# A hybrid decoder trunk on one core: the first mixer's triangular inverses with both token halves in turns over four quadrants of TensorE, their masks on GpSimd

## The chip, the core and the metric

One Trainium2 chip, one of its cores. The time is the device time of one launch in microseconds. The kernel before has a median of 1386.16 us over three runs (1382.22 to 1388.61).

## What is computed

The reference is a two-layer decoder trunk on 256 tokens of width 1024, all in float32. Layer 0 has a hybrid mixer: an RWKV-7 head group (8 heads of 64) and a sparse-attention head group (8 query heads, compressed, selected and sliding-window branches), whose outputs are joined and projected. Layer 1 has a Mamba-2 mixer. After each mixer comes a mixture of experts (32 experts of width 512, each token goes to two), and after all a final norm. The change touches the RWKV group only:

```python
def step(state, inp):                       # per token, per head
    r_t, w_t, k_t, v_t, a_t, b_t = inp
    sa = jnp.einsum('bhij,bhj->bhi', state, a_t)
    state = state * w_t[:, :, None, :] + sa[..., None] * b_t[:, :, None, :] + v_t[..., None] * k_t[:, :, None, :]
    return state, jnp.einsum('bhij,bhj->bhi', state, r_t)
...
y = y * gn_w + gn_b
bonus = jnp.sum(r_h * k_h * r_k, -1, keepdims=True) * v_h
y = y.astype(cols.dtype) + bonus.reshape(b_, s_, RWKV_WIDTH)
return y * g
```

## The kernel before

The kernel has one block per stage: `hyb` (the first mixer), experts of layer 0, `ssm` (the Mamba-2 mixer), experts of layer 1, the final norm. In a block each engine has its own stream of instructions, written out by hand; `at(...)` turns the name of a mark into a semaphore and a count, and an engine waits for it. There is no planner: the order of the calls is the order on the engine.

**The recurrence in chunks.** RWKV's recurrence is done in four chunks of 64 tokens (two per half of 128 tokens, `t`, and in it `q` = 0 or 1). For each chunk and head a strictly lower triangular 64x64 matrix N comes from a and b, and (1 - N) is inverted. There are 2 halves x 8 heads = 16 slots (`slot(t, e, c)`, head 2c + e), and in each slot chunk q lies in partitions 64q to 64q + 63 (`at64(q)`). `tri` (in `amt`) is the inverse as grown so far, `triT` (in `kk`) its transpose, both 128 x 16 x 64. Level 0 comes from the masks `lev0` and `levT`; each of the five levels l = 1 to 5 then doubles the blocks: `products(l)` (PE) multiplies `lv` (the level's masked part of N, `masked`, L799) with `tri` into `prod`; ACT copies `prod` out of PSUM (`products_read`, L1057); `grown(l)` on PE multiplies `triT` with `prod` (dT) and `prod` with `triT` (dTT, both in `squares`, L1360), and `grown(l)` on DVE adds them to `tri` and `triT` (L810). The last level has no dT.

**On PE** a matmul of 64 x 64 uses one quadrant of the array: its rows go by the partitions of the inputs, its columns by those of the output. In `squares` both are `at64(q)`, so a run of them uses two quadrants, on the diagonal. `against` (L1322, for `bar` and `kar`) and the `nn` matmuls (L1334) read at `at64(e)` and write at `at64(q)`. The profile has two records for each float32 matmul and one for a transpose.

**In turns with attention.** The attention group's selected and window branches are eight units i = 0 to 7 (`UNITS`; 128 keys wide for i = 0 to 3, 256 for i = 4 to 7). Unit i goes: `scores(i)` on PE (L1242), `scores(i)` on DVE (scale and mask L626, maximum L631), `exps(i)` on ACT (L938, four heads), `weighted(i)` on DVE (reciprocal L640, L641, product L644), `weights_turned(i)` on PE (transposes, L1155), `weights_read(i)` on ACT (L948), and for each pair of units `attended` on PE (L1265). Level l and unit l share a stretch, in this order on each engine (levels 3 to 5 alike but for akv, the turned compressed weights and attended):

```python
# PE, level 4                          # DVE                        # ACT
weights_turned(4)                      scores(5)                    attention_read(0)
scores(5)                              masked(4)                    weights_read(4)
products(4)                            pre = pre * gate             products_read(4)
grown(4)                               weighted(5)                  exps(5)
                                       grown(4)
```

PSUM has eight banks: attention takes its jobs from banks 0 to 2 in turn (`inner`), the inverse from banks 4 to 7 (`right`); `take` (L189) hands out the next bank of the pool and waits until its last job has been read. DVE also builds `pre` (bonus times v, plus `gn_b`, times the gate; L826, L834, L842) and scales `gate` by `gn_w` (L847).

After level 5 come `wu` (L1443; the inverse times its right sides, copied by ACT for e = 0 and by DVE for e = 1), `gains` (L1454, L1456) and `queries` (L1465), the step from chunk to chunk (`step`, `carried`), the group norm on DVE, and the join: on PE the output projection in 64 matmuls of 512 columns (L1535 for the attention half, L1544 for the RWKV half after `turnr`).

**DMA.** SP loads the experts' weights of layer 0 ahead into a ring of 24 slots of 1 MB, as the mixer's buffers come free: it waits for `gup`, `attended(3)`, `qs(1, 1)` and `turnr(1)` in turn (L565 to L576), and in the experts' block for the router. GpSimd has no work in this block; in `ssm` it has 14 instructions (L2302, L2310, L2312).

## Time and profile before

| | us |
|---|---|
| median of three runs | 1386.16 |
| the profiled execution | 1384.46 |
| its span (first to last instruction) | 1382.7 |
| PE busy | 1252.7 (91%) |
| DVE busy | 408.8 (30%) |
| ACT busy | 269.8 (20%) |
| GpSimd (POOL) busy | 15.2 (1%) |
| DMA, bytes moved | 464 MB, mean 336 GB/s |

The page also cuts the span into 40 slices of 34.6 us. The first mixer takes slices 1 to 7; DMA is busy in nine tenths of the time or more in slices 8 to 20 and 29 to 40, the two expert stages, and in few tenths in most of slices 2 to 6. PE is the modelled busy time of matmuls, PEld that of weight loads, PEclk the TensorE clock that was granted (1.00 is 2.4 GHz, 0.50 is 1.2 GHz). An "idle before" with an arrow names what ended an engine's wait.

### The profile page before, as it was taken

The numbers are of one execution on the slowest core, as the hardware profiler recorded it, in microseconds if no ns is written. First come the engines' busy times: TensorE is split into PE (matmuls) and PEld (weight loads), VectorE is DVE, ScalarE is ACT, GpSimd is POOL, SyncE is SP. The second block draws the span as 40 slices with busy tenths as digits, with TensorE's granted clock in tenths as the row PEclk, the third lists the DMA queues.
The fourth block names the chain that finished last, engine by engine and source line by source line (L and its number), as shares of the span: only waits on it lengthen the run. The fifth ranks groups of instructions, "written<-read, shape, count | busy, mean of one in ns | idle before, by whom it ended". The sixth has DMA issues, their size and how long they took to land. (4 is left out here: it accounts for less than half of the span.)

```text
span 1382.7 us, 20783 instructions
## 1 busy us (share of the span) xinstructions
PE 1252.7 (91%) x8752; PEld 701.5 (51%) x8752; DVE 408.8 (30%) x1019; ACT 269.8 (20%) x537; POOL 15.2 (1%) x18
## 2 busy tenths in 40 slices
PE   7999999899999888598899999998999998877986
PEld 4678874444444433243378888544444453333432
DVE  1158764511112111112135756224211211110211
ACT  2241440311110100010132566112111010000101
POOL 0000000000000000000000111000000000000000
PEclk9999999999999999889999999999999999997999
DMA  9620128999999999999964455958999999999996
GB/s 305 189 95 28 64 82 354 404 428 428 428 425 429 427 427 427 426 426 428 369 219 169 152 212 199 366 230 327 427 428 427 428 427 428 427 426 426 427 428 264
DMA packets 63482, 464.08 MB, mean 336 GB/s; under 512 B 8272, under 2 KB 13680, under 8 KB 34960
## 3 DMA queue, kind: packets, MB, share of 16 engines
q1 hardware_dynamic: 63376, 462.61, 81.8%
q8 instruction: 73, 1.20, 0.4%
q14 instruction: 33, 0.27, 0.1%
HBM read 461.51 MB, written 1.08 MB: 335 GB/s over the span
## 5 line engine op out<-in xcount | busy, mean ns | idle before, releaser
L1982 PE MATMUL bank<-raw,xg 128*32 128x512 f32 x1664 | 233.6, 654 | 46.9 <-DMA raw<-in_moe_w_up 41.1
L1892 DVE TENSOR_TENSOR aT<-bank,sg 128x128 f32<-128x128 f32 (+1 forms) x64 | 20.2, 316 | 553.9 <-ACT sg L1803 553.9
L1982 PEld LDWEIGHTS bank<-raw,xg 128*32 128x32 f32 x1664 | 57.9, 119 | 196.6 <-issue 122.0
L1919 PE MATMUL bank<-sel,ux 128*128 128x64 f32 (+1 forms) x896 | 117.7, 287 | 17.0 <-DVE sel L1825 16.1
L1919 PEld LDWEIGHTS bank<-sel,ux 128*128 128x128 f32 x896 | 110.9, 202 | 40.7 <-issue 21.6
L2029 PE MATMUL sums<-ys,selT 64*128 64x512 f32 x512 | 127.2, 615 | 3.3 <-DVE ys L1905 3.3
L1800 ACT COPY gus<-bank 128x512 f32<-128x512 f32 x64 | 37.5, 586 | 439.5 <-PE bank L1982 332.1
L2020 PE MATMUL bank<-raw,aT 128*32 128x512 f32 x832 | 100.0, 598 | 10.8 <-DVE aT L1892 10.8
L2029 PEld LDWEIGHTS sums<-ys,selT 64*128 64x128 f32 x512 | 44.1, 186 | 87.8 <-issue 80.9
L1963 PE MATMUL bank<-raw,xg 128*64 128x512 f32 x384 | 87.0, 594 | 0.0
L2623 PE MATMUL sums<-uT,wr 128*128 128x256 f32 x352 | 78.1, 380 | 0.0
L1905 DVE COPY ys<-bank 128x512 f32<-128x512 f32 x64 | 44.0, 688 | 111.6 <-PE bank L2020 79.8
L1993 PEld LDWEIGHTS bank<-cst,gus 128*128 128x128 f32 x416 | 50.3, 191 | 44.5 <-issue 34.9
L2623 PEld LDWEIGHTS sums<-uT,wr 128*128 128x128 f32 x352 | 66.3, 190 | 9.4 <-issue 0.7
L1993 PE MATMUL bank<-cst,gus 128*128 128x64 f32 x416 | 57.5, 281 | 4.2 <-ACT gus L1800 4.2
L1774 ACT COPY xg<-bank 128x256 f32<-128x256 f32 (+1 forms) x56 | 23.4, 418 | 177.9 <-PE bank L1919 177.9
L1963 PEld LDWEIGHTS bank<-raw,xg 128*64 128x64 f32 x384 | 32.2, 137 | 49.2 <-issue 44.9
L2623 PE MATMUL bank<-uT,wr 128*128 128x256 f32 x256 | 57.1, 381 | 0.0
L2623 PEld LDWEIGHTS bank<-uT,wr 128*128 128x128 f32 x256 | 48.0, 190 | 6.9 <-issue 0.7
L2020 PEld LDWEIGHTS bank<-raw,aT 128*32 128x32 f32 x832 | 21.7, 109 | 50.6 <-issue 30.4
L2007 PE MATMUL bank<-raw,aT 128*64 128x512 f32 x192 | 43.8, 598 | 3.0 <-DVE aT L1892 3.0
L1803 ACT ACTIVATE sg<-bank 128x128 f32<-128x128 f32 (+1 forms) x64 | 19.1, 298 | 137.7 <-PE bank L1993 114.8
(414 smaller groups left out, 1282.4 us busy)
## 6 DMA issues: line engine op xcount, KB each, us to landing
raw<-in_moe_w_gate SPq DMA_DIRECT2D x54, 2048.0 KB, 41.7
raw<-in_moe_w_up SPq DMA_DIRECT2D x54, 2048.0 KB, 46.1
raw<-in_moe_w_down SPq DMA_DIRECT2D x54, 2048.0 KB, 45.0
raw<-in_moe_w_gate SPq DMA_DIRECT2D x20, 1024.0 KB, 11.2
raw<-in_moe_w_up SPq DMA_DIRECT2D x20, 1024.0 KB, 12.7
raw<-in_moe_w_down SPq DMA_DIRECT2D x20, 1024.0 KB, 12.4
wr<-in_ssm_w_in SPq DMA_DIRECT2D x10, 2048.0 KB, 8.1
wr<-in_hyb_w_in SPq DMA_DIRECT2D x5, 2048.0 KB, 7.9
```

Source lines behind the costliest of these rows:

```text
L1774: nc.scalar.copy(dst[:, :, 4 * half:4 * half + 4, :].rearrange("p x k s -> p k x s"), bank[SIDE_BANK][:, 0:8 * n].rearrange("p (k x s) -> ...
L1800: nc.scalar.copy(gus[:, :, :], bank[GU_BANK][:, :].rearrange("p (q j) -> p j q", j=4)).then_inc(S["gus"], 1)
L1892: V.tensor_tensor(out, bank[TURN_BANK][:, 0:8 * n].rearrange("p (j x) -> p j x", j=4)[:, :, n:2 * n], gated, ALU.mult).then_inc(S["act"], 1)
L1905: V.tensor_copy(ys[:, :], bank[Y_BANK][:, :]).then_inc(S["y"], 1)
L1919: i = T.matmul(bank[SIDE_BANK][:, k * n:(k + 1) * n].rearrange("p (x s) -> p x s", x=2), ux[:, t, 4 * half + k, :], src[:, t, :, :], start ...
L1963: i = T.matmul(bank[GU_BANK][CAP * m:CAP * m + CAP, :], xg[:, odd, k, :], raw[:, slot, (k % 4) * FH:(k % 4 + 1) * FH], start=(k == 0), sto ...
L1982: i = T.matmul(bank[GU_BANK][CAP_S * c:CAP_S * c + CAP_S, :], xg_f[:, x, 4 * half + k, :], raw[:, slot, k * FH:(k + 1) * FH], start=(half ...
L1993: i = T.matmul(bank[TURN_BANK][:, j * CAP:(j + 1) * CAP], gus[:, j, :], C("ident64"), start=True, stop=True)
L2007: i = T.matmul(bank[Y_BANK][CAP * n:CAP * n + CAP, :], aT[:, j, :], raw[:, slot, jj * D + n * BANK:jj * D + (n + 1) * BANK], start=(j == 0 ...
L2020: i = T.matmul(bank[Y_BANK][CAP_S * c:CAP_S * c + CAP_S, :], aT_s[:, 2 * half + jj, :], raw[:, slot, jj * D + n * BANK:jj * D + (n + 1) * ...
L2029: i = T.matmul(bank[ACC[2 * t + n]][:, :], selT[CAP * n:CAP * n + CAP, x, t * P:(t + 1) * P], ys[CAP * n:CAP * n + CAP, :], start=False, s ...
L2623: i = T.matmul(b[:, c * SEQ:(c + 1) * SEQ], wr2[:, n % 3, k, (2 * j + c) * P:(2 * j + c + 1) * P], uT2[:, k, :], start=(k == 0), stop=(k = ...
```

## The change

Both halves' matmuls now alternate. `tri` stays where it is for both halves; for the second half `triT`, `prod`, the a side and akv lie in the other 64 partitions (chunk q in `at64(1 - q)`). Then `products` and dT use two quadrants for the first half and the other two for the second; dTT keeps to the diagonal for both. The second half of `triT` starts from new matmuls (`crossed`), and at(1) is formed by matmuls with the identity. `products(l)` now stands first in its stretch on PE and `products_read(l)` ahead of `weights_read(l)` on ACT. akv, wu, gains and queries alternate likewise. DVE adds both dT ahead of both dTT. The masks and the steps of `pre` and `gate` go to GpSimd; SP and DVE wait for its last (`gain`). The diff, cut to its core:

```diff
             sp.wait_ge(*at("attended", 3))
+            sp.wait_ge(*at("gain"))
             load_ahead(sp, 0, hyb_fed, hyb_attended)
...
             go(V.tensor_tensor(lv[:, 1], nrb[:, :, 0, :], rep(levT[:, 1], SL), ALU.mult), "lvl", 1)
-            did(V.tensor_tensor(triT, nrb[:, :, 0, :], rep(levT[:, 0], SL), ALU.mult))
+            go(V.tensor_tensor(triT[:, 0:HEADS, :], nrb[:, 0:HEADS, 0, :], rep(levT[:, 0], HEADS), ALU.mult))
+            dve.wait_ge(*at("crossed"))
+            for e in range(2):
+                go(V.tensor_tensor(triT[:, slot(1, e, 0):slot(1, e, 4), :],
+                                   bank_of("crossed", e)[:, 0:4 * CHK].rearrange("p (c s) -> p c s", s=CHK),
+                                   rep(levT[:, 0], 4), ALU.mult), "read", "crossed", e)
+            dve.wait_ge(dve_done, DV.n)
...
             def grown(l):

-                for g in range(2):
-                    for name, dst in (("dT", tri), ("dTT", triT)):
-                        if name == "dT" and l == LAST:
-                            continue
+                for name, dst in (("dT", tri), ("dTT", triT)):
+                    if name == "dT" and l == LAST:
+                        continue
+                    for g in range(2):
                         dve.wait_ge(*at(name, l, g))
                         sl = dst[:, HEADS * g:HEADS * g + HEADS, :]
                         go(V.tensor_tensor(sl, bank_of(name, l, g)[:, :].rearrange("p (c s) -> p c s", s=CHK), sl,
...
             weighted(1)

             scores(2)
-            masked(1)
             compressed_turned(0)
             weighted(2)
             grown(1)

             scores(3)
...
-            masked(2)
-            dve.wait_ge(*at("read", "bon"))
...
             weighted(3)
...
             scores(4)
-            masked(3)
-            dve.wait_ge(*got("par"))
...
             compressed_turned(1)
             weighted(4)
...
             scores(6)
-            go(V.tensor_tensor(gate[:, :, :], gate[:, :, :], rep(gn_w, HALVES), ALU.mult))
             weighted(6)
             grown(5)
...
+            dve.wait_ge(*at("gain"))
...
+        @block.gpsimd
...
+            def masked(l):
+
+                pool.wait_ge(*(at("prod", l - 1, 1) if l > 1 else at("lvl", 1)))
+                go(G.tensor_tensor(lv[:, (l + 1) % 2], nrb[:, :, 0, :], rep(levT[:, l + 1], SL), ALU.mult), "lvl", l + 1)
+
+            masked(1)
+            pool.wait_ge(*at("read", "bon"))
+            pool.wait_ge(*at("read", "vt", 1))
+            heads_ = lambda ap: ap.rearrange("p t (n i) -> p (t n) i", i=HD)
+            go(G.tensor_tensor(heads_(pre), heads_(vt), rep(bon[:, :, :].rearrange("p t n -> p (t n)"), HD, 2), ALU.mult))
+            masked(2)
+            pool.wait_ge(*got("par"))
+            pool.wait_ge(pool_done, PO.n)
+            go(G.tensor_tensor(pre, pre, rep(gn_b, HALVES), ALU.add))
+            masked(3)
+            pool.wait_ge(*at("read", "gup", 1))
+            pool.wait_ge(pool_done, PO.n)
+            go(G.tensor_tensor(pre, pre, gate[:, :, :], ALU.mult))
+            masked(4)
+            pool.wait_ge(pool_done, PO.n)
+            go(G.tensor_tensor(gate[:, :, :], gate[:, :, :], rep(gn_w, HALVES), ALU.mult), "gain")
...
             def products_read(l):

                 for g in range(2):
-                    act.wait_ge(*at("prod", l, g))
+                    act.wait_ge(*at("prod", l, 1))
                     if l > 1:
-                        act.wait_ge(*at("dTT", l - 1, g))
+                        act.wait_ge(*at("dTT", l - 1, 1))
                     A.copy(prod[:, HEADS * g:HEADS * g + HEADS, :],
                            bank_of("prod", l, g)[:, :].rearrange("p (c s) -> p c s", s=CHK)).then_inc(
...
             by_slot("at", xr_[:, :, 0, :], 1)
+            products_read(1)
             weights_read(1)
-            products_read(1)
...
             pe.wait_ge(*at("rt"))
             against("bar", bh)
+            bs = [take(pe, "crossed", e, pool=right) for e in range(2)]
+            for c in range(4):
+                for e in range(2):
+                    for q in range(2):
+                        i = T.matmul(bs[e][at64(1 - q), c * CHK:(c + 1) * CHK],
+                                     bh[at64(e), c, chunk(1, q)], ar[at64(e), c, 0, chunk(1, q)], start=True, stop=True)
+            i.then_inc(pe_done, PE.one(("crossed",)))
             pe.wait_ge(*at("rk"))
             b = take(pe, "bon", pool=right)
...
-            for t in range(HALVES):
-                turned(("at", t), [ar[:, c, 0, tok(t)] for c in range(4)], right)
-
...
+            turned(("at", 0), [ar[:, c, 0, tok(0)] for c in range(4)], right)
+            b = take(pe, "at", 1, pool=right)
+            for c in range(4):
+                for q in range(2):
+                    i = T.matmul(b[at64(1 - q), c * P:(c + 1) * P], ar[:, c, 0, chunk(1, q)], ident, start=True,
+                                 stop=True)
+            i.then_inc(pe_done, PE.one(("at", 1)))
...
+            def squares(bs, left_, right_, source, to):
+
+                for n in range(HEADS):
                     for q in range(2):
-                        i = T.matmul(b[at64(q), s * CHK:(s + 1) * CHK], left_[at64(q), HEADS * g + s, :],
-                                     right_[at64(q), HEADS * g + s, :], start=True, stop=True)
+                        for g in bs:
+                            i = T.matmul(bs[g][at64(to(g, q)), n * CHK:(n + 1) * CHK],
+                                         left_[at64(source(g, q)), HEADS * g + n, :],
+                                         right_[at64(source(g, q)), HEADS * g + n, :], start=True, stop=True)
                 return i
+
+            straight = lambda g, q: q
+            crossed = lambda g, q: q if g == 0 else 1 - q

             def products(l):

                 pe.wait_ge(*at("lvl", l))
                 if l == 1:
                     pe.wait_ge(*at("triT0"))
+                else:
+                    pe.wait_ge(*at("read", "dT", l - 1, 1))
+                bs = {g: take(pe, "prod", l, g, pool=right) for g in range(2)}
+                squares(bs, lv[:, l % 2], tri, straight, crossed).then_inc(pe_done, PE.one(("prod", l, 1)))
+                new[("prod", l, 0)] = new[("prod", l, 1)]
+
+            def grown(l):
+
+                pe.wait_ge(*at("read", "prod", l, 1))
+                if l > 1:
+                    pe.wait_ge(*at("read", "dTT", l - 1, 1))
+                if l < LAST:
+                    bs = {g: take(pe, "dT", l, g, pool=right) for g in range(2)}
+                    squares(bs, triT, prod, crossed, straight).then_inc(pe_done, PE.one(("dT", l, 1)))
+                    new[("dT", l, 0)] = new[("dT", l, 1)]
                 for g in range(2):
-                    if l > 1:
-                        pe.wait_ge(*at("read", "dTT", l - 1, g))
-                    squares(take(pe, "prod", l, g, pool=right), g, lv[:, l % 2], tri).then_inc(
-                        pe_done, PE.one(("prod", l, g)))
-
-            def grown(l):
-
-                for g in range(2):
-                    pe.wait_ge(*at("read", "prod", l, g))
-                    for name, left_, right_ in (("dT", triT, prod), ("dTT", prod, triT)):
...
-                        squares(take(pe, name, l, g, pool=right), g, left_, right_).then_inc(
-                            pe_done, PE.one((name, l, g)))
-
+                    squares({g: take(pe, "dTT", l, g, pool=right)}, prod, triT, crossed, crossed).then_inc(
+                        pe_done, PE.one(("dTT", l, g)))
+
+            products(1)
             weights_turned(1)
             scores(2)
-            products(1)
             pe.wait_ge(*at("zz", 11))
             for t in range(HALVES):
                 turned(("vt", t), [v4[:, c, tok(t)] for c in range(4)], right)
             compressed_turned(0)
             grown(1)
...
+
+            products(2)
             attended(0)
-
             weights_turned(2)
             scores(3)
-            products(2)
             compressed_out(0)
...

+            products(3)
             weights_turned(3)
             scores(4)
-            products(3)
             pe.wait_ge(*at("read", "vt", 1))
             pe.wait_ge(*at("read", "kar", 1, 1))
-            for t in range(HALVES):
-                b = take(pe, "akv", t, pool=right)
...
+            bs = [take(pe, "akv", t, pool=right) for t in range(HALVES)]
+            for e in range(2):
+                for c in range(4):
+                    for q in range(2):
+                        for t in range(HALVES):
+                            i = T.matmul(bs[t][at64(crossed(t, q)), (4 * e + c) * HD:(4 * e + c + 1) * HD],
                                          akr[at64(q), slot(t, e, c), 0, :], vt[at64(q), t, head(e, c)],
                                          start=True, stop=True)
-                i.then_inc(pe_done, PE.one(("akv", t)))
+            i.then_inc(pe_done, PE.one(("akv", 1)))
+            new[("akv", 0)] = new[("akv", 1)]
...
             grown(3)
+
+            products(4)
             attended(1)
-
             weights_turned(4)
             scores(5)
-            products(4)
             grown(4)
...
             compressed_out(1)
             pe.wait_ge(*at("read", "akv", 1))
             pe.wait_ge(*at("read", "at", 1))
...
+            pe.wait_ge(*at("read", "dTT", LAST, 1))
+            for e in range(2):
+                bs = [take(pe, "wu", t, e, pool=right) for t in range(HALVES)]
+                for c in range(4):
+                    for q in range(2):
+                        for t in range(HALVES):
+                            half = at64(crossed(t, q))
+                            i = T.matmul(bs[t][at64(q), 2 * c * CHK:2 * (c + 1) * CHK], triT[half, slot(t, e, c), :],
+                                         flat(xr_[half, slot(t, e, c), :, :], "x", "s"), start=True, stop=True)
+                i.then_inc(pe_done, PE.one(("wu", 1, e)))
+                new[("wu", 0, e)] = new[("wu", 1, e)]
+
+            def gains_queries(j):

                 t, q = j // 2, j % 2
-                b = take(pe, "g", j, pool=right)
+                t2, q2 = (j + 1) // 2, (j + 1) % 2
+                b, b2 = take(pe, "g", j, pool=right), take(pe, "qm", j + 1, pool=right)
                 for c in range(4):
                     for e in range(2):
...
                         o = b[at64(e), c * HD:(c + 1) * HD]
                         T.matmul(o, nrb[at64(q), slot(t, e, c), 2, :], wu[at64(q), slot(t, e, c), 1, :], start=True,
                                  stop=False)
+                        T.matmul(b2[at64(e), 2 * c * CHK:2 * (c + 1) * CHK], wu[at64(q2), slot(t2, e, c), 0, :],
+                                 flat(nrb[at64(q2), slot(t2, e, c), 1:3, :], "x", "s"), start=True, stop=True)
                         i = T.matmul(o, kt[at64(q), t, head(e, c)], vt[at64(q), t, head(e, c)], start=False, stop=True)
                 i.then_inc(pe_done, PE.one(("g", j)))
...
+                new[("qm", j + 1)] = new[("g", j)]
...
-            gains(1)
+            gains_queries(0)
             pe.wait_ge(*at("read", "wu", 1, 0))
             pe.wait_ge(*at("read", "wu", 1, 1))
-            gains(2)
-            queries(2)
-            queries(3)
+            gains_queries(1)
+            gains_queries(2)
             weights_turned(7)
```

## Rows read from the trace of the kernel before

**Rows 1.** stretches: us, busy us (records) per engine, PEclk, DMA share, GB/s
```profile
206.00:210.00 4.00, 2.04 (x68) 1.93 (x67) 2.24 (x5) 1.87 (x2) 0.00 (x0) 0.97 0.97 393
210.00:214.00 4.00, 4.00 (x29) 2.25 (x25) 3.76 (x9) 0.30 (x1) 0.00 (x0) 0.60 1.01 428
...
230.00:234.00 4.00, 4.00 (x10) 1.66 (x9) 0.69 (x1) 0.00 (x0) 0.00 (x0) 1.00 0.18 76
...
340.00:380.00 40.00, 39.75 (x268) 18.91 (x266) 5.63 (x15) 4.62 (x10) 0.00 (x0) 1.00 1.00 426
```

**Rows 2.** PE in order of time: start us, us, instruction, records, idle before
```profile
138.97 2.08 PE L1360 MATMUL sums<-amt,wr 64*64 64x64 f32 x64
...
158.56 2.08 PE L1360 MATMUL sums<-amt,wr 64*64 64x64 f32 x64
...
168.30 1.09 PE L1155 MATMUL bank<-cst,pr 128*128 128x128 f32 x8
169.73 1.13 PE L1242 MATMUL bank<-kT,qT 64*128 64x256 f32 x8 [0.33 <-ACT pT L948]
170.79 2.08 PE L1360 MATMUL sums<-amt,wr 64*64 64x64 f32 x64
...
177.37 1.09 PE L1155 MATMUL bank<-cst,pr 128*128 128x128 f32 x8 [0.77 <-DVE pr L644]
...
186.41 1.09 PE L1155 MATMUL bank<-cst,pr 128*128 128x128 f32 x8 [0.73 <-DVE pr L644]
...
189.90 3.71 PE L1443 MATMUL sums<-wr,kk 64*64 64x128 f32 x64
...
199.09 1.09 PE L1155 MATMUL bank<-cst,pr 128*128 128x128 f32 x8
...
210.89 11.67 PE L1535 MATMUL bank<-zz,qk 128*128 128x512 f32 x24
```

**Rows 3.** DVE in order of time, units 3 and 5 and the adds
```profile
149.19 0.75 DVE L626 SCALAR_TENSOR_TENSOR pr<-bank,cst_hyb 128x256 f32<-128x256 f32 x2 [1.39 <-PE bank L1242]
...
153.69 0.69 DVE L644 TENSOR_TENSOR pr<-pr,den 128x512 f32<-128x512 f32 x1
...
170.96 1.29 DVE L626 SCALAR_TENSOR_TENSOR pr<-bank,cst_hyb 128x512 f32<-128x512 f32 x2 [2.27 <-PE bank L1242]
172.28 1.22 DVE L631 TENSOR_REDUCE nmx<-pr 128x4 f32<-128x1024 f32 x1
...
176.09 1.23 DVE L644 TENSOR_TENSOR pr<-pr,den 128x1024 f32<-128x1024 f32 x1
177.23 0.68 DVE L810 TENSOR_TENSOR amt<-sums,amt 128x512 f32<-128x512 f32 x1
```

**Rows 4.** ACT in order of time: the first exponential of units 3 and 5 (one of four each)
```profile
151.60 0.40 ACT L938 ACTIVATE pr<-pr,nmx 128x128 f32<-128x128 f32 x1
...
173.54 0.51 ACT L938 ACTIVATE pr<-pr,nmx 128x256 f32<-128x256 f32 x1
```

**Rows 5.** PE in order of time: `nn` and `bar`, 32 matmuls each
```profile
116.46 1.16 PE L1334 MATMUL sums<-qk,front 64*64 64x64 f32 x64
...
125.09 1.98 PE L1322 MATMUL sums<-front,qk 64*64 64x128 f32 x64
```

**Rows 6.** groups by line, 130 to 260 us: records, busy us, mean ns, idle before
```profile
L1155 PE MATMUL bank<-cst,pr 128*128 128x128 f32 x44 | 6.6, 289 | 1.5 <-DVE pr L644 1.5
...
L1265 PE MATMUL bank<-pT,nsav 128*64 128x512 f32 x24 | 6.0, 609 | 0.0
...
L1242 PE MATMUL bank<-kT,qT 64*128 64x128 f32 x16 | 1.4, 297 | 0.0
```

**Rows 7.** GpSimd's lines in `ssm`: count, shortest/median/longest ns, first and last start
```profile
L2310 POOL TENSOR_TENSOR sq<-sq x3: 1264/1267/1671, 825.1 to 862.8; 128x512 f32<-128x512 f32 x3
...
L2302 POOL TENSOR_TENSOR front<-front,dtv x8: 1043/1090/1221, 759.8 to 835.8; 128x512 f32<-128x512 f32 x8
```

**Rows 8.** one of DVE's lines in `ssm`, alike; and it in time beside GpSimd's 759.85 to 762.13
```profile
L2348 DVE SCALAR_TENSOR_TENSOR xs__2453<-xr,feat,xs__2453 x48: 475/483/1261, 741.8 to 802.4; 128x256 f32<-128x256 f32 x48
...
761.15 1.26 DVE L2348 SCALAR_TENSOR_TENSOR xs__2453<-xr,feat,xs__2453 128x256 f32<-128x256 f32 x1
```

56 lines of the change are left out of this document (10 added, 46 removed).

## The prediction

> **What bounds the kernel now.** I read the page first. Its slices show DMA at nine tenths nearly everywhere but in the first mixer; the stretches of four and forty microseconds [rows 1] then say what a shift of the mixer is worth. At 230 to 234 us the DMA share is only 0.18: the ring's next loads wait for the transposes late in the mixer (`turnr`). Later, at 340 to 380 us, DMA stands at 1.00 and PE at 39.75 of 40. So the expert stage begins when the mixer ends and cannot make time up: I count a shift of the mixer's last join one to one in the kernel's end. In the join itself PE streams 512-wide matmuls without a gap from 210.89 us [rows 2]; everything before it counts by how it moves that start.
>
> Second, PE in order of time through the five levels [rows 2]. Levels 1 to 3 are PE's: products to products takes (158.56 - 138.97) / 2 = 9.8 us in levels 1 and 2 and 12.2 us in level 3, with no idle noted in front. Levels 4 and 5 are not: PE waits 0.77 us for DVE's `pr` before `weights_turned(5)` and 0.73 before `weights_turned(6)`. There the attention units set the period, 177.37 - 168.30 = 9.07 and 186.41 - 177.37 = 9.04 us: transposes 1.09, 0.33 for ACT to free a bank, scores 1.13, DVE scores and maximum 2.5, four exponentials 2.1, DVE weights 1.6 [rows 2, 3, 4], 8.8, and the hand-overs are the rest. The inverse's matmuls fit inside that chain. This is what I rest the forecast on.
>
> **The change, part by part.**
>
> *Four quadrants.* A level's products (64 records, 2.08 us [rows 2]) now alternate over both halves. The nearest row is `nn`, also 64 records of 64x64 whose rows go by e and columns by q: 1.16 us [rows 5]. The bounds are 1.16 (it behaves as `nn`) and 2.08 (nothing overlaps); I take 1.1, since operands and shape are `nn`'s. dT gets the same; dTT of each half stays in two quadrants. So PE sheds about 0.95 + 0.95 a level, 0.95 in level 5, 0.95 in akv, 1.7 in wu (3.71 us [rows 2] against 2.0 as `bar` with its 128 columns [rows 5]) and some 1.8 where gains and queries interleave: about 13 us in all. Added are `crossed` (32 records, 0.5 us) and, for at(1), eight matmuls of 128 columns in place of four transposes, 0.35 us. The Trainium skill, TensorE: Matmul & The Clock Gate, Part 1, says that matmuls never start closer than about 25 ns; by that floor 64 records would take 1.6 us, and each level would keep 1 us more of PE. `nn` disagrees: 1160 / 64 = 18 ns [rows 5].
>
> *The order on PE.* `products(l)` moves ahead of `weights_turned(l)`, and it waits for the two dT adds of the level before. DVE does those adds after `weighted(l)`. Queued behind products on PE are attended, weights_turned and scores; DVE, then ACT, then DVE again wait for those. The chain of a level is now a ring with everything in it: products 1.1, weights_turned, scores, DVE scores, exponentials, weights, two adds 1.2 [rows 3], products. For levels 1 and 2, 128 wide: 1.1 + 0.6 + 0.7 + 1.4 + 1.5 + 1.0 + 1.2 = 7.5 [rows 3, 4, 6], with hand-overs, v's copies in front of the exponentials in the first and attended(0) 1.0 [rows 6] in the second, 8.2 and 9.0. Level 3: 1.1 + 0.6 + 1.13 + 2.5 + 2.1 + 1.6 + 1.2 = 10.3. Level 4: attended(1) is behind products too, 1.1 + 1.0 + 1.09 + 0.33 + 1.13 + 2.5 + 2.1 + 1.6 + 1.2 = 12.1 with hand-overs, against 9.07. From products(5) to weights_turned(6) there are no adds, 10.1. Products(1) would start near 138.2 (before, weights_turned(1) stood there; crossed, at(1) and the later reads of kar put back 0.7). Sum: 138.2 + 8.2 + 9.0 + 10.3 + 12.1 + 10.1 = 187.9 for weights_turned(6), against 186.41: +1.5. The first three levels gain what PE sheds, the last two give it back.
>
> *Tail.* From weights_turned(6), PE reaches wu after 189.90 - 186.41 = 3.5 us, then needs 2.0 for it. ACT's wu copies end at about 5.8, exponentials (7) at 7.9, weights (7) at 9.6. Then gains_queries(2) needs banks that DVE reads only after weighted(7) (S and mt of 1): +1.0, and +1.05 for itself; weights_turned(7) starts 11.7 after weights_turned(6), against 12.68 [rows 2]: -1.0. So the earlier PE work is hidden by the exponentials again. Order alone: +0.5 us; the hand-overs leave it open by 1.5 either way.
>
> *Masks and gains on GpSimd.* DVE loses four masks and four more 1024-wide steps, each as long as a 256-wide unit's weights, 1.23 us [rows 3]. In levels 3 and 4 they stood in the time in which DVE waits for the exponentials, so their going is worth nothing. On GpSimd 512 wide takes 1.26 (1.09 with a repeated operand) [rows 7], so a 1024-wide one some 2.3. Eight of them are 18 us, done long before they are needed: each mask has a level's time, and `gain`, on which SP's load of the second stretch of slots now waits too, is ready some 35 us before attended(3), the wait ahead of it. But DVE's 128x256 with two SBUF inputs takes 0.483 us as a rule and 1.26 at most, and the 1.26 us ones lie beside GpSimd's work [rows 8]: DVE stands until the GpSimd instruction ends. That hits triT + ident64 (behind level 2's mask, 1.6 us; a little of it comes back if the transposes after it run at full clock, I take 0.8) and the weights of units 2 and 3, which meet the run of pre, mask, pre, mask, pre from v's copies on (5 x 2.3 = 11.5 us). Each waits between nothing and two whole instructions, 4.6; I take 1.05 each, about half of one. Together +2.9, bounds 0 and 10. No row shows GpSimd beside a DVE add that reads PSUM: those adds cost between nothing and 2.3 us a level. I take nothing, as for them there is one SBUF input. The Trainium skill, SBUF — State Buffer, Who interferes with whom, says that a DVE instruction with at most one SBUF input does not contend. By it only the 2.9 stand; were every DVE instruction held, 5 more.
>
> *The clock.* PE will stand idle where it did not: after dTT(4) until products(5), some 4.6 us, and before weights_turned(6), 2.6 us (both are the ring's 12.1 and 10.1 less PE's own 7.5). After PE had been busy 2.04 of 4 us the granted clock was 0.60 over the next four [rows 1], some 3.2 us of them at 1.2 GHz. What PE then does (products, weights_turned, scores) is on the ring and takes double: 1.6 us lost a time, +3.2 together; bounds 0 and 7 (the clock may fall elsewhere in the levels too).
>
> The remaining edits have one answer. triT in three parts costs DVE 0.3 us; ACT reads products before weights, at equal length; adds of dT before dTT let products go 1.2 us earlier, counted above; akv is one wait. Cover for all is the ring; without it they are tenths.
>
> **Sum**: 0.5 + 2.9 + 3.2 = +6.6 us, taken as +7. The profiled execution took 1384.46 us (span 1382.7); the median of the runs shown is 1386.16, 1.7 above it and within their spread. Forecast 1391.5 us. A measurement of this kernel tells 0.5%, 7 us, from no change, so the forecast stands on that line.
>
> **Rivals.**
> - *PE was the bound and stays it*: the ring's wait has slack, and the 13 us shed less 1 added arrive in the mixer. For: no idle before PE in levels 1 to 3. Against: the waits for `pr` in levels 4 and 5. It needs weighted(l) to be finished a whole products before PE gets there. 1384.5 - 12 = 1372.5 us; half of it gives 1378. Chance 0.13, for both.
> - *Order alone*: GpSimd's instructions miss DVE's two-input ones and the clock stays up or falls only where nothing waits: +0.5, 1385 us; with one of the two, 1388. For: half of a GpSimd instruction is a small wait, and no row shows how little idleness between 2 us in 4 and none lowers the clock. Chance 0.31.
> - *Quadrants do not overlap, or DVE is held for every GpSimd instruction*: the change does not do what it says. Products and dT then keep 2.08 in the ring, 5 x 0.95, or the adds wait: +5 on top, 1397 us. Against: `nn`. Chance 0.10.
>
> **How the numbers follow.** The forecast has 0.46; its bounds reach further up than down, so 0.31 of it lies above the line of 0.5% and 0.15 below. Slower by over 0.5%: 0.31 and the last rival's 0.10, 0.41. Within: 0.31 + 0.15 = 0.46. Faster: 0.13. The range leaves out the first rival's faster part (0.12) and the upper end of the bounds (0.06): 1381 to 1400 us; the likeliest case's own is 1387 to 1397.
>
> **What would show it.** In the changed trace: products at about 1.1 us (else the quadrants failed); products(4) to products(5) near 12 us with PE idle some 4.6 us behind DVE's dT adds (if it is 9, the ring is wrong and the time falls); DVE's weights of units 2 and 3 or triT + ident64 longer than 1.22 us beside GpSimd; granted clock under 1 in 175 to 200 us; gains_queries(2) waiting for DVE. A join start before 210.89 us would make the prediction wrong in sign.

## The result and the profile after

| | before | after |
|---|---|---|
| median, us | 1386.04 (1382.22 to 1388.61) | 1391.45 (1389.81 to 1393.97) |
| runs | 6 | 6 |
| the profiled execution, us | 1384.46 | 1393.75 |
| its span, us | 1382.7 | 1391.9 |
| PE busy, us | 1252.7 | 1250.3 |
| GpSimd busy, us | 15.2 | 34.2 |

The ratio of after to before is 1.0045, with a 95% interval from 1.0028 to 1.0062: 5.4 us slower by the medians, against a forecast of 1391.5 us. The profiled execution of after lies near the top of its runs (1393.75), so its span exaggerates the difference (+9.2): 3.6 us of that come up behind the start of the join. The distance from the start of `bar` to the start of the join leaves them out. PE's busy time differs so little in the table for the same reason: between these two marks it fell from 78.4 to 69.5 us, and behind them it is 6.5 us higher.

PE in order of time in the kernel after (start us, us, instruction, records, idle before). L1390 is `squares`: `sums<-amt,wr` is `products`, `sums<-kk,kp` is dTT. L1172 with `bank<-cst,pr` is `weights_turned`, L1482 `wu`, L1566 the join:

```profile
125.23 1.98 PE L1339 MATMUL sums<-front,qk 64*64 64x128 f32 x64
...
135.82 1.97 PE L1172 MATMUL sums<-cst,qk 128*128 128x128 f32 x8
...
139.47 1.16 PE L1390 MATMUL sums<-amt,wr 64*64 64x64 f32 x64
...
149.80 1.19 PE L1390 MATMUL sums<-amt,wr 64*64 64x64 f32 x64 [3.10 <-DVE amt L808]
...
159.00 1.16 PE L1390 MATMUL sums<-amt,wr 64*64 64x64 f32 x64
...
167.11 2.08 PE L1390 MATMUL sums<-kk,kp 64*64 64x64 f32 x64 [2.14 <-ACT wr L1101]
...
169.60 1.16 PE L1390 MATMUL sums<-amt,wr 64*64 64x64 f32 x64 [0.41 <-DVE amt L808]
...
182.02 1.98 PE L1390 MATMUL sums<-amt,wr 64*64 64x64 f32 x64 [4.81 <-DVE amt L808]
183.94 1.97 PE L1172 MATMUL bank<-cst,pr 128*128 128x128 f32 x8
...
193.56 1.09 PE L1172 MATMUL bank<-cst,pr 128*128 128x128 f32 x8 [2.63 <-DVE pr L645]
...
197.05 1.98 PE L1482 MATMUL sums<-wr,kk 64*64 64x128 f32 x64
...
205.16 1.09 PE L1172 MATMUL bank<-cst,pr 128*128 128x128 f32 x8
...
216.47 12.26 PE L1566 MATMUL bank<-zz,qk 128*128 128x512 f32 x24
```

Three things are to be seen here. The quadrants do what was meant: products took 2.08 us before [rows 2] and take 1.16 now, `wu` 3.71 before and 1.98 now. Yet the join starts 216.47 - 125.23 = 91.2 us after `bar`, against 210.89 - 125.09 = 85.8 before [rows 2, 5]: 5.4 us later, as the medians say (by the ratio it is 6.2). And PE now waits for DVE in front of products, 4.81 us at the longest. The groups by line of the same kernel, 130 to 205 us (records, busy us, mean ns, idle before), say how much of that there is in all:

```profile
L1390 PE MATMUL sums<-amt,wr 64*64 64x64 f32 x320 | 6.7, 240 | 8.3 <-DVE amt L808 8.3
...
L1172 PE MATMUL bank<-cst,pr 128*128 128x128 f32 x36 | 6.1, 314 | 2.6 <-DVE pr L645 2.6
```

The first row is what the new order brought: 8.3 us in which PE had nothing to do but wait for the adds of dT. Before, none of the rows of products shows a wait [rows 2]. It is not all the order's doing: of the 3.10 us in front of products(2), 2.2 go when GpSimd no longer holds DVE (part 3).

DVE and GpSimd in order of time, same kernel, one fence for each:

```profile
132.42 2.59 DVE L792 TENSOR_TENSOR kk<-kk,cst 128x1024 f32<-128x1024 f32 x1
...
145.66 2.80 DVE L645 TENSOR_TENSOR pr<-pr,den 128x512 f32<-128x512 f32 x1
148.38 1.27 DVE L808 TENSOR_TENSOR amt<-sums,amt 128x512 f32<-128x512 f32 x2
```

```profile
131.20 2.73 POOL L912 TENSOR_TENSOR wr<-z,cst_hyb 128x1024 f32<-128x1024 f32 x1 [130.75 <-DVE wr L784]
...
145.56 2.35 POOL L912 TENSOR_TENSOR wr<-z,cst_hyb 128x1024 f32<-128x1024 f32 x1
148.06 2.63 POOL L922 TENSOR_TENSOR uT<-uT,par 128x1024 f32<-128x1024 f32 x1
```

`triT + ident64` (L792) takes 2.59 us instead of 1.2: it ends 135.01 - 133.93 = 1.1 us after GpSimd's mask does, as if it had only then begun. The weights of unit 2 (L645) take 2.80 in place of 0.69 [rows 3], beside level 3's mask. The two adds right behind them take 1.27 together, their usual time, though GpSimd works from 148.06 to 150.69: one of their inputs is in PSUM, and they are not held. So the rule that the prediction took from the Trainium skill (SBUF — State Buffer, Who interferes with whom: a DVE instruction with at most one SBUF input does not contend) agrees with this trace. Whether a hold also costs time is another question, which part 3 answers.

The clock and the ring of loads, in stretches of four and forty us of the kernel after (columns as in [rows 1]):

```profile
178.00:182.00 4.00, 0.00 (x0) 0.01 (x1) 2.89 (x6) 1.01 (x5) 0.00 (x0) 0.65 0.00 0
182.00:186.00 4.00, 3.98 (x74) 3.55 (x74) 1.07 (x2) 1.67 (x4) 0.00 (x0) 0.50 0.01 4
...
190.00:194.00 4.00, 1.37 (x10) 0.49 (x7) 2.07 (x4) 1.83 (x8) 0.00 (x0) 1.00 0.00 0
...
238.00:242.00 4.00, 3.33 (x11) 1.56 (x10) 0.69 (x1) 0.59 (x1) 0.00 (x0) 1.00 0.11 16
...
340.00:380.00 40.00, 39.59 (x259) 17.91 (x260) 8.52 (x26) 4.03 (x9) 0.00 (x0) 1.00 1.00 426
```

The long wait was followed by 1.2 GHz, the shorter one before `weights_turned(6)` was not. The pause of DMA before `turnr`'s loads comes later too: by stretches of 1 us the DMA share is 0.00 from 232 to 235 us before and from 238 to 241 us after. The expert stage later is as saturated as before, so the lateness of the mixer is passed on.

### The profile page after: what moved, and what is told of

It is laid out like the page before. It is cut to its first block and busy times, and to the rows that moved or that the text cites. A ratio compares the mean times of both kernels' runs of the same rounds, so it can differ in the third digit from the quotient of the medians.

```text
span 1391.9 us, 20879 instructions
## 1 busy us (share of the span) xinstructions
PE 1250.3 (90%) x8796; PEld 693.4 (50%) x8796; DVE 403.3 (29%) x1013; ACT 269.1 (19%) x537; POOL 34.2 (2%) x26
## 5 line engine op out<-in xcount | busy, mean ns | idle before, releaser
L1950 PE MATMUL bank<-sel,ux 128*128 128x64 f32 (+1 forms) x896 | 117.7, 287 | 16.1 <-DVE sel L1856 15.2
L2051 PE MATMUL bank<-raw,aT 128*32 128x512 f32 x832 | 101.4, 605 | 10.8 <-DVE aT L1923 10.8
## 6 DMA issues: line engine op xcount, KB each, us to landing
raw<-in_moe_w_down SPq DMA_DIRECT2D x20, 1024.0 KB, 12.2
```

Of the source, the lines that this page charges most:

```text
L1950: i = T.matmul(bank[SIDE_BANK][:, k * n:(k + 1) * n].rearrange("p (x s) -> p x s", x=2), ux[:, t, 4 * half + k, :], src[:, t, :, :], start ...
L2051: i = T.matmul(bank[Y_BANK][CAP_S * c:CAP_S * c + CAP_S, :], aT_s[:, 2 * half + jj, :], raw[:, slot, jj * D + n * BANK:jj * D + (n + 1) * ...
```

## The experiments

The runs came in three batches on three chips, each against the kernel before on the same chip (medians 1384.37, 1385.32 and 1384.99 us). Ratios are to that kernel; 0.001 is 1.4 us. "From `bar` to the join" is read from each profile like the 91.2 and 85.8 above; the last two columns compare each version with the kernel before, by that distance in one execution and by the ratio of the times:

| version | part | from `bar` to the join, us | by it | by the ratio |
|---|---|---|---|---|
| the kernel after | | 91.2 | +5.4 | +6.2 |
| old order | 1 | 84.0 | -1.8 | -3.7 |
| masks on DVE | 1 | 92.3 | +6.5 | +6.9 |
| both back, and its repeat | 1, 5 | 82.1, 81.4 | -3.7, -4.4 | -5.5, -5.1 |
| the kernel before, GpSimd's part | 1 | 88.7 | +2.9 | +2.8 |
| after, halves in line | 2 | 98.6 | +12.8 | +12.2 |
| both back, halves in line | 2 | 84.4 | -1.4 | -1.8 |
| GpSimd timed | 3 | 89.5 | +3.7 | +4.0 |
| nine and five fillers | 4 | 97.3 | +11.5 | +10.8 |
| four and two fillers | 4 | 91.7 | +5.9 | +4.3 |
| old order in levels 4 and 5 | 5 | 85.0 | -0.8 | -0.3 |
| old order, GpSimd timed | 5 | 81.4 | -4.4 | -4.3 |

In every version the two agree within 2 us: a shift of the join counts one to one. It also says how far one profile can be trusted; effects of a microsecond or two need both columns.

### 1. Each part back by itself, and both

The old order on PE and ACT, everything else as after (levels 2 to 5 alike):

```diff
-            products(1)
             weights_turned(1)
             scores(2)
+            products(1)
...
-            products_read(1)
             weights_read(1)
+            products_read(1)
```

> The changed kernel, but products(l) stands behind scores(l + 1) on PE again, and ACT reads weights before products, as before the change; four quadrants and GpSimd stay. Theory (the order makes a ring of products, attention and adds): levels 4 and 5 fall from 12.4 and 11.5 us to some 9.1, PE's two long idle stretches close, no half clock at 182 to 186 us; join start from 216.5 to about 208 us, time about 1383. Rival (GpSimd's holds on DVE are the cost, the order only shifts PE's work): join start stays above 214 us, time 1389 or more. Rival (what PE sheds has no value anywhere): about 1386, the time before the change.

Measured: 1382.56 us, ratio 0.9973 (0.9958 to 0.9989). The other part, masks and the steps of `pre` and `gate` back on DVE in the new order:

```diff
             scores(2)
+            masked(1)
             compressed_turned(0)
...
             scores(3)
+            masked(2)
+            dve.wait_ge(*at("read", "bon"))
+            dve.wait_ge(*at("read", "vt", 1))
+            go(V.tensor_tensor(heads_(pre), heads_(vt), rep(bon[:, :, :].rearrange("p t n -> p (t n)"), HD, 2),
+                               ALU.mult))
             weighted(3)
```

> The changed kernel, but masks, pre and gate are made by DVE again, at their places before the change; the order on PE stays. Theory (GpSimd's holds cost 2.9 us by the prediction, 1.4 + 2.2 by the changed trace; DVE's own extra work fits under the exponentials): triT + ident64 1.22 us, weights of unit 2 0.69 us, products(5) as late behind the adds as before; time 1388 to 1389, join start 213 to 214. Rival (the order alone is the cost): 1391. Rival (DVE is short of time): slower than 1391, as DVE gets 8 x 1.2 us back.

Measured: 1392.32 us, 1.0050 (1.0034 to 1.0065): no shorter than with GpSimd, where 1388 to 1389 was expected. Both edits together:

> Four quadrants alone: the order of before and the masks on DVE, the layout and the interleaved matmuls of the change. Theory: the four-quadrant matmuls shed PE work in levels 1 to 3, where PE was the bound, and nothing in 4 and 5, where the attention units set the period of 9.05 us; both costs are gone: join start about 206 us, time about 1381, some 5 us under before. Rival (quadrants give nothing, since each level waits for DVE and ACT anyway): 1386.

Measured: 1380.53 us, 0.9960 (0.9944 to 0.9975). And the reverse, the kernel before with only the eight steps moved to GpSimd:

```diff
+        @block.gpsimd
+        def _(pool):
...
+            masked(1)
+            pool.wait_ge(*at("read", "bon"))
+            pool.wait_ge(*at("read", "vt", 1))
...
             sp.wait_ge(*at("attended", 3))
+            sp.wait_ge(*at("gain"))
```

> The kernel before, with only masks, pre and gate moved to GpSimd. Theory: DVE is held at triT + ident64 (1.4 us, on the way to kar and the transposes, so on the path) and at one or two of the units' weights (up to 2.4 us each, where PE is the bound partly hidden); DVE's relief is worth little: 1387 to 1389. Rival (the move helps, since DVE is nearly full in level 4): 1384. Rival (no effect): 1386.

Measured: 1387.66 us, 1.0020 (1.0007 to 1.0033). Its trace holds the weights of units 2 and 3 both (DVE, in order of time):

```profile
147.79 2.80 DVE L645 TENSOR_TENSOR pr<-pr,den 128x512 f32<-128x512 f32 x1
...
156.81 2.88 DVE L645 TENSOR_TENSOR pr<-pr,den 128x512 f32<-128x512 f32 x1
```

What follows: the order is what makes the kernel slow. With it undone the time falls by 0.0072, 10 us, and below that of the kernel before; with the masks on DVE in both, it is worth 1.0050 - 0.9960 = 0.0090, 12.5 us. GpSimd's part costs 0.0020 in the kernel before (2.8 us); in the old order with quadrants the difference is 0.0013 and the intervals overlap, though the profiles say 2 to 3 us (84.0 against 82.1 and 81.4). In the new order, taking it away gained nothing: DVE's own steps came into the ring instead. Level 1 became 1.7 us shorter (8.65 for 10.33), and levels 2 and 3, where DVE now worked without a pause from its scores to its adds, 0.6 and 1.2 us longer. PE waited for the adds 1.62 us before products(4) (PE, masks on DVE; 0.41 in the kernel after):

```profile
169.57 1.16 PE L1381 MATMUL sums<-amt,wr 64*64 64x64 f32 x64 [1.62 <-DVE amt L817]
```

### 2. The quadrants by themselves

Same layout, same instructions, but the halves one after the other in `squares`, so that each run of matmuls keeps to two quadrants:

```diff
-                for n in range(HEADS):
-                    for q in range(2):
-                        for g in bs:
+                for g in bs:
+                    for n in range(HEADS):
+                        for q in range(2):
```

> The changed kernel with the loop over the halves outside in squares: same matmuls, same layout, but the halves' matmuls one after the other, two quadrants at a time. Theory (in the new order products stands in the ring of each level): products 2.08 instead of 1.16, the five levels longer by 0.9 each, dT's 0.9 only where grown ends late; 1395 to 1396. Rival (PE has so much idle time now that the quadrants no longer matter): 1391.5. Rival (the quadrants never overlapped): products stay at their length.

Measured: 1398.84 us, 1.0088 (1.0067 to 1.0109). The same edit in the version with both parts back:

> Four quadrants taken out of the kernel that has the order and the masks of before: halves one after the other in squares (akv, wu, gains and queries still alternate). Theory (in the old order PE is the bound in levels 1 to 3, so products and dT cost 1.9 us a level there and nothing in levels 4 and 5): 1380.5 + 5 = 1385 to 1386. Rival (what helps there is akv, wu and gains with queries): stays at 1381.

Measured: 1383.41 us, 0.9987 (0.9973 to 1.0001). PE, new order with the halves in line, products(1) and products(5):

```profile
138.91 1.91 PE L1390 MATMUL sums<-amt,wr 64*64 64x64 f32 x64
...
184.45 3.32 PE L1390 MATMUL sums<-amt,wr 64*64 64x64 f32 x64 [4.23 <-DVE amt L808]
```

1.91 against 1.16 us at full clock, from nothing but the order in which the same 32 matmuls are issued: the overlap is in the turns. It is worth 1.0088 - 1.0045 = 0.0043 (6 us) where products stand in the ring and 0.9987 - 0.9960 = 0.0027 (4 us, where 5 were expected) where they do not; both are differences between batches. What is left of the quadrants without `squares` (akv, wu, gains and queries) is 0.0013, not clear of noise. The first figure is too large for the ring alone. From products(1) to `weights_turned(6)` the five levels are 4.6 us longer (58.7 for 54.1), the 0.9 a level that was expected. Another 3.7 us come up in the tail, where `squares` has no part but the granted clock was 0.50 from 198 to 206 us and `wu` took 3.69 us instead of 1.98.

### 3. GpSimd's steps at other moments

```diff
+            pool.wait_ge(*at("triT0"))
             masked(1)
+            masked(2)
+            pool.wait_ge(*at("weighted", 2))
             pool.wait_ge(*at("read", "bon"))
...
-            masked(2)
+            masked(3)
+            pool.wait_ge(*at("weighted", 3))
             pool.wait_ge(*got("par"))
```

> The changed kernel with GpSimd's eight instructions at other times: the first mask waits for triT + ident64, each step of pre for the weights of the unit before it, so that none should lie beside a DVE instruction with two SBUF inputs; DVE's own work stays as light as in the changed kernel. Theory (holds cost 1.4 + 2.2 us on the path, of which up to a microsecond may sink into other waits): triT + ident64 back at 1.22, weights of unit 2 at 0.69; products(5) some 3 us earlier, time 1388 to 1389. Rival (the holds cost nothing, as putting the work back on DVE did not shorten the kernel): 1391.5.

Measured: 1389.71 us, 1.0029 (1.0015 to 1.0044). DVE in order of time, then PE from the transposes in front of products(1) to products(2), and GpSimd:

```profile
130.03 1.23 DVE L792 TENSOR_TENSOR kk<-kk,cst 128x1024 f32<-128x1024 f32 x1
...
141.95 0.69 DVE L645 TENSOR_TENSOR pr<-pr,den 128x512 f32<-128x512 f32 x1
```

```profile
133.36 1.09 PE L1176 MATMUL sums<-cst,qk 128*128 128x128 f32 x8
...
135.84 1.16 PE L1394 MATMUL sums<-amt,wr 64*64 64x64 f32 x64
...
143.99 1.21 PE L1394 MATMUL sums<-amt,wr 64*64 64x64 f32 x64 [0.90 <-DVE amt L808]
```

```profile
131.34 2.36 POOL L912 TENSOR_TENSOR wr<-z,cst_hyb 128x1024 f32<-128x1024 f32 x1 [130.89 <-DVE kk L792]
137.12 2.37 POOL L912 TENSOR_TENSOR wr<-z,cst_hyb 128x1024 f32<-128x1024 f32 x1 [3.42 <-PE sums L1394]
```

Both holds are gone. Level 1 took 143.99 - 135.84 = 8.15 us in place of 149.80 - 139.47 = 10.33: the hold on unit 2's weights cost what it lasted, 2.2 us. From `bar` to products(1) it was 13.0 in place of 14.2, and that is not the hold on triT + ident64. The transposes behind it start 133.36 - 122.85 = 10.5 us after `bar` here and 135.82 - 125.23 = 10.6 in the kernel after; PE was still busy with `kar` while DVE was held. What differs is their clock, 1.09 us against 1.97. A trace with the same hold and the higher clock (part 4, the second version; its `bar` is at 125.10) shows the same:

```profile
135.53 1.25 PE L1172 MATMUL sums<-cst,qk 128*128 128x128 f32 x8 [0.23 <-DVE wr L796]
```

Products(1) starts 13.2 us after `bar` in it. So of the 1.2 us about 1.0 is clock and 0.2 the hold, and the two holds together cost 2.4 us of the 3.5 that they last. By time it is 1.0045 - 1.0029 = 0.0016, 2.2 us (the two intervals overlap). This execution had its clock fall twice later on, and products(5) and `weights_turned(6)` took 1.99 and 1.97 us.

### 4. PE kept busy while it waits

```diff
             scores(5)
             grown(4)
+            filler(9)
...
             attended(2)
+            filler(5)
             weights_turned(6)
```

A filler is a matmul of 512 columns from constants into a free bank, whose result is never read.

> The changed kernel with PE kept busy in its two long idle stretches: nine matmuls of 512 columns ahead of products(5), five ahead of weights_turned(6), into a bank that is free; their results are overwritten. Theory (the half clock costs some 1.8 us of the added time): clock 1.00 at 178 to 190 us, products(5) 1.16 instead of 1.98, weights_turned(5) 1.09 instead of 1.97, time 1389.5 to 1390. Rival (the clock takes nothing from the end, since DVE and ACT set the pace): 1391.5 as without. Rival (fillers overrun the wait): later than without, 1392 or more.

Measured: 1396.53 us, 1.0078 (1.0058 to 1.0098). The fillers had been priced at half of what they take: a float32 matmul of 512 columns leaves two records and took 0.89 us, so nine of them stood in the way for 7.99 us where 4.8 were free. So this run prices a level that is some 4 us too long (16.4 for 12.4), and not the clock. Once more with four and two:

> The changed kernel with 4 matmuls of 512 columns between dTT(4) and products(5) and 2 before weights_turned(6), at 0.89 us each as measured: 3.6 us in the hole of 4.8, 1.8 in the one of 2.6, so that they end before the adds do. Their results are never read. Theory A (the idle stretch lowers the clock and that costs about 1.8 to 3.2 us): products(5) at 1.16 us, weights_turned(5) at 1.09, ratio 1.002 to 1.0035, join start 2 to 3 us sooner after bar than the changed kernel's 91.2. Rival (the clock falls elsewhere or what it costs is hidden by the exponentials): ratio 1.0045 as before, within 0.0015.

Measured: 1389.40 us, 1.0031 (1.0017 to 1.0045). PE in order of time, then the stretches:

```profile
148.68 1.98 PE L1397 MATMUL sums<-amt,wr 64*64 64x64 f32 x64 [3.09 <-DVE amt L808]
...
169.82 1.99 PE L1397 MATMUL sums<-amt,wr 64*64 64x64 f32 x64
...
178.41 3.70 PE L1390 MATMUL bank<-cst 128*128 128x512 f32 x8
183.29 1.16 PE L1397 MATMUL sums<-amt,wr 64*64 64x64 f32 x64 [1.18 <-DVE amt L808]
184.39 1.09 PE L1172 MATMUL bank<-cst,pr 128*128 128x128 f32 x8
186.22 1.13 PE L1259 MATMUL bank<-kT,qT 64*128 64x256 f32 x8 [0.74 <-ACT pT L965]
...
193.83 1.09 PE L1172 MATMUL bank<-cst,pr 128*128 128x128 f32 x8 [0.69 <-DVE pr L645]
```

```profile
166.00:170.00 4.00, 2.65 (x71) 2.49 (x74) 3.08 (x6) 1.76 (x6) 0.00 (x0) 0.85 0.00 0
170.00:174.00 4.00, 4.00 (x76) 2.77 (x75) 0.87 (x2) 1.98 (x4) 0.00 (x0) 0.72 0.02 4
...
178.00:182.00 4.00, 4.00 (x26) 1.78 (x20) 1.79 (x5) 2.07 (x8) 0.00 (x0) 1.00 0.00 0
182.00:186.00 4.00, 2.30 (x73) 1.91 (x72) 2.34 (x4) 1.49 (x4) 0.00 (x0) 1.00 0.01 4
```

With PE busy in the hole, products(5) and `weights_turned(5)` ran at full clock, and products(5) to `weights_turned(6)` took 10.54 us instead of 11.54. So a fall of the clock there costs 1.0 us and not the 1.7 that the two instructions lose: at full clock PE waits 0.74 for ACT to free a bank. (Where `weights_turned(6)` was slow too, in part 3, the same stretch took 11.91.) But the clock fell elsewhere in this execution. It fell behind the 3.09 us wait before products(2), which took 1.98 (1.19 in the kernel after), and level 2 was 10.5 us in place of 9.2; and behind the 2.14 us wait for ACT before dTT(3) (0.85 and 0.72, products(4) at 1.99), and level 4 was 13.5 in place of 12.4. In the kernel after the same two waits left the clock at 1.00. So the join, expected 2 to 3 us sooner, starts 91.7 us after `bar`, no sooner than the 91.2 of the kernel after. By time the version is 0.0014, 2 us, below the kernel after; that fits both the theory (1.002 to 1.0035) and the rival (within 0.0015 of 1.0045), and the intervals overlap. The price of one fall is shown; that the fillers save anything is not.

### 5. Where the order costs, and what is best

Products first in levels 1 to 3 only, the old order in levels 4 and 5, masks on DVE:

> Masks and gains on DVE; products first in levels 1 to 3, and the old order in levels 4 and 5 alone. Theory A (the forecast's ring: products first costs only where attention sets the period, levels 4 and 5; 8.2, 9.0 and 10.3 us for levels 1 to 3 are no longer than PE's own): the same as with all five levels in the old order, ratio 0.995 to 0.998, levels 4 and 5 at 9 to 9.5 us. Rival (the loss is spread over all levels, each add of dT on the ring): half of the 11.8 us between the two orders stays, ratio about 1.000. In both the granted clock stays at 1.00 between 174 and 190 us, since PE's idle stretch is gone.

Measured: 1384.33 us, 0.9998 (0.9985 to 1.0012). A repeat of both parts back on the same chip:

> The changed kernel with both the old order and the masks and gains back on DVE, once more: a repeat, as the base of the next runs. If the first measurement (ratio 0.9960 to before) holds, 0.995 to 0.997, about 5 us faster than before. If it was luck of one chip, 0.999 to 1.001. The join starts 82 to 83 us after the start of bar in the first case, 85 to 86 in the second.

Measured: 1380.33 us, 0.9963 (0.9952 to 0.9975). Of the 0.0087 between this and the new order in all levels (1.0050, from the first batch), levels 1 to 3 cost 0.0035 (4.9 us) and levels 4 and 5 0.0052 (7.2 us). The expectation that the first three levels cost nothing fell; the rival, that about half stays, held. `weights_turned` of units 3 to 6 in the version with products first in levels 1 to 3 (PE in order of time), then the same rows of the repeat, with dTT(3):

```profile
158.14 0.66 PE L1163 MATMUL bank<-cst,pr 128*128 128x128 f32 x4
...
169.59 1.23 PE L1163 MATMUL bank<-cst,pr 128*128 128x128 f32 x8
...
178.80 1.09 PE L1163 MATMUL bank<-cst,pr 128*128 128x128 f32 x8 [1.20 <-DVE pr L645]
...
187.83 1.09 PE L1163 MATMUL bank<-cst,pr 128*128 128x128 f32 x8 [0.24 <-DVE pr L645]
```

```profile
156.49 0.66 PE L1163 MATMUL bank<-cst,pr 128*128 128x128 f32 x4
...
163.52 2.08 PE L1381 MATMUL sums<-kk,kp 64*64 64x64 f32 x64 [0.90 <-ACT wr L1092]
...
166.54 1.09 PE L1163 MATMUL bank<-cst,pr 128*128 128x128 f32 x8
...
175.61 1.09 PE L1163 MATMUL bank<-cst,pr 128*128 128x128 f32 x8 [1.20 <-DVE pr L645]
...
184.65 1.09 PE L1163 MATMUL bank<-cst,pr 128*128 128x128 f32 x8 [0.25 <-DVE pr L645]
```

From unit 3 to unit 4 it is 11.45 us with products first and 10.05 without; from 4 to 6 it is 18.24 and 18.11. Levels 1 and 2 together (`weights_turned(1)` to `(3)`) took 18.5 and 15.8. The waits of PE say why. In the repeat PE has none in levels 1 and 2 (0.62 us once in the first version) and 0.90 us in level 3: there it is still PE that bounds, and what it shed arrives. With products first the same levels have 1.41 and 0.34 us in front of products(2) and (3), 0.69 in front of dTT(2) and 2.14 in front of dTT(3), 4.6 us in all, for DVE's adds and for ACT, which is behind its exponentials. (Some tenths of the 11.45 are clock: it was granted at 0.57 from 166 to 170 us.) So the old order leaves levels 1 and 2 to PE and levels 4 and 5 to attention, and products first ties the two together in every level.

Last, the old order with GpSimd timed as in part 3, as a candidate:

> Old order on PE and ACT, GpSimd's work kept, but each step of it set where DVE has no instruction with two SBUF inputs. Theory A (only the moment of GpSimd's work costs): DVE is as free as with nothing on GpSimd, and DVE's own steps lay in its waits for the exponentials: the same as with both parts back, within 0.1% of it, ratio 0.995 to 0.997. Rival (taking 8 steps off DVE is worth something once nothing is held): 2 us below it, 0.994 or less. Second rival (GpSimd costs in other ways, through later masks or its hand-overs): 2 to 4 us above it, 0.998 to 1.000, as with the old order and GpSimd not timed (0.9973).

Measured: 1380.21 us, 0.9969 (0.9956 to 0.9981). As with the masks on DVE, within the interval: once nothing is held, it does not matter where the eight steps are. (Against the untimed version of part 1, 0.9973, the time shows nothing either; only the profiles differ, 81.4 us from `bar` to the join against 84.0.) On the two traces `weights_turned(3)` to `(6)` take the same 28.1 us, with DVE busy or not: DVE's steps fitted into its waits for the exponentials.

The best version therefore is quadrants for the matmuls, the old order and the masks on DVE: 0.9960 and 0.9963 on two chips, 4 to 5 us faster than the kernel before by the medians of their batches (1380.53 against 1384.37, 1380.33 against 1384.99) and 11 to 12 us faster than the change by the ratios. The version with GpSimd timed cannot be told from it.

## Why the prediction was right

The mechanism is right: PE waits where the forecast put the waits, and nearly as long (4.81 us before products(5), 4.6 forecast; 2.63 before `weights_turned(6)`, 2.6 forecast). That 1391.5 and 1391.45 agree is luck. The forecast added 7 us to the 1384.46 of one execution; the measured step is 5.4, from a median of 1386.04. A step 1.6 us too large stands on a base 1.6 us too low. Inside the step errors cancel as well:

| term, us | forecast | measured |
|---|---|---|
| order, to `weights_turned(6)` | +1.5 | +3.7 |
| holds | +2.9 | +2.3 |
| clock | +3.2 | +1.0 |
| tail | -1.0 | -1.6 |
| sum | +6.6 | +5.4 |

- **A shift of the mixer's join counts one to one.** Right: +5.4 us at the join, +5.4 in the medians, and within 2 us in every version above.
- **Quadrants.** Products 1.16 us, as `nn` and not at 25 ns a record: 64 records in 1.16 us is 18 ns each. The floor of about 25 ns that the Trainium skill gives (TensorE: Matmul & The Clock Gate, Part 1) does not hold for these; `wu` was foreseen at 2.0 and took 1.98.
- **The ring.** Forecast for levels 1 to 5: 8.2, 9.0, 10.3, 12.1, 10.1 us. Measured: 10.3, 9.2, 10.6, 12.4, 11.5; without holds (part 3) level 1 is 8.15, without the half clock (part 4) level 5 is 10.54. Every one is within 0.5 us of its forecast; together they are 1.2 us above it (50.9 for 49.7). In level 2 products(3) shows no wait, so there the trace does not show the adds as the bound.
- **The start.** The mis-sized part of the order's term. Forecast for products(1) 138.2 - 125.09 = 13.1 us after `bar`, which is 0.7 more than before. In the first version with both parts back, without a hold and with the transposes as slow as before, `weights_turned(1)` takes this place and starts 139.15 - 125.00 = 14.15 us after `bar`, 1.7 more. `kar` took 3.69 us there and in the kernel after, against 2.47 before. With the five levels it makes 14.15 + 50.9 - 61.3 = +3.7.
- **Holds on GpSimd's account.** Forecast 2.9 us: 0.8 for triT + ident64, 1.05 each for the weights of units 2 and 3. They last 2.59 - 1.22 = 1.4, 2.80 - 0.69 = 2.1 and nothing, and cost 0.1 (14.24 - 14.15), 2.2 and nothing; by time, 2.2 (part 3) and 2.8 (in the kernel before, where the hold on triT + ident64 did reach PE: its wait in front of the transposes was 4.15 us, against 1.64). The sum came out near by luck: one hold cost nothing, one cost twice its share, one did not occur. That unit 3 escapes is no accident of one execution. In all four traces with products first and GpSimd not timed, GpSimd's step ends 1.0 to 1.6 us before these weights start; in the kernel before it holds them (2.88 us).
- **The clock.** Forecast 3.2 us for two falls; in the profile of after there was one on the ring, and it cost 1.0, since the wait for ACT's bank covers the rest. In other executions the second fell too. This term was too large by 2 us in this profile.
- **Tail.** `weights_turned(6)` to `(7)`: forecast 11.7, measured 205.16 - 193.56 = 11.60, and `gains_queries(2)` waited 1.98 us for DVE's `cum` at 204.07. From there to the join 11.3, against 11.8 before, half a microsecond not forecast.

To `weights_turned(6)` the forecast is 1.5 + 2.9 + 3.2 = 7.6, and 68.3 - 61.3 = 7.0 is measured from `bar`; less 1.6 in the tail, 5.4.

What the prediction did not price is what its term "order alone, +0.5" is made of. It is a difference: the change without its order and without GpSimd brings 5 us (0.9960; it still has the new layout and DVE's adds of dT ahead of dTT), the order with its idle stretches and their clock takes 12 (0.0090). The rival "PE was the bound and stays it" (1372.5 or 1378 us) is excluded by the time, and even with the old order only part arrives. PE's busy time between `bar` and the join fell from 78.4 us to 68.2, about 10 us where the forecast had 12, and the join came 4.4 us sooner (both in the repeat of part 5): levels 1 to 3 are 4.7 us shorter, levels 4 and 5 and the tail are not. And its sentence that the first three levels gain what PE sheds was true only against the kernel before: against the same quadrants in the old order they lose 4.9 us (part 5). These three levels were PE's own, as the forecast had read, and products first made them wait for DVE and ACT.

That DVE's steps are worth nothing off DVE was right in the old order (part 5), and wrong in the new one: there they are in the ring of levels 2 and 3 (0.6 and 1.2 us, part 1), and the masks on GpSimd earn back what their holds cost (1.0045 against 1.0050).

## What to carry to other kernels

Where two chains of work share an in-order engine, look stretch by stretch which of them sets the period, and after the change as well as before it. Making one cheaper pays only where it was the bound. An instruction moved ahead "because it is short" brings its own wait into the other chain, with all that is queued behind it. Take matmuls of 64x64 in turns over all four quadrants, wherever two independent sets exist and the layout can put them on different quadrants; but let the work that waits last stand last. If elementwise work goes to GpSimd, start it where DVE reads PSUM or waits, and not because GpSimd is idle; and price a hold by whether its engine was the one waited for, not by how long it lasts. When a forecast comes out to a tenth of a microsecond, check its terms before believing it.

## What the runs showed of the chip that was not expected

- GpSimd's own time stretches as well: its mask takes 2.36 us alone and 2.73 beside DVE's instructions on `triT` (3.25 in the kernel before with GpSimd's part), the step of `pre` 2.63 beside the held weights.
- The same wait of PE of 2.14 us, at the same place in the program, left the granted clock at 1.00 in one execution and brought 0.85 and 0.72 in another; a wait of 2.63 us likewise, and one of 3.1 us in front of products(2). The forecast's fixed price for a hole can be right only on average.
- The same 32 matmuls of 64x64 take 1.16 us in turns over four quadrants (1.98 at half clock) and 1.91 us one half after the other (3.32 at half clock).
- A hold of 1.4 us on DVE cost 0.1 to 0.2 us where PE was busy anyway, and one of 2.1 us cost 2.2 where PE waited for DVE.
